# Reciprocal square roots in fewer operations, and the decay output's root and gate applied from PSUM: a two-block transformer kernel in float32 on one core

## The chip, the cores and the metric

One core of one Trainium2 chip. The time is the device time of one execution in microseconds (us). Of the kernel before there are three timed runs and one profiled execution, whose rows are shown further down.

## The reference

A hidden state of 512 tokens by 1024 goes through two blocks of two layers each, all in float32. A layer of the first block is cut here to what the change touches:

```python
def _rms(x, g=None):
    y = x * lax.rsqrt(jnp.mean(x * x, axis=-1, keepdims=True) + EPS)
    return y if g is None else y * g

h = _rms(x, norm_g[l])
proj = h @ w_in[l]                       # 9304 columns, split into the parts
...
o = jnp.einsum('bnchk,bnhkv->bnchv', q, states)      # decay branch: 4 heads of 128
o = _rms(o, norm_g)                                  # gain gla_norm_g[l], 128 numbers
y_a = o * jax.nn.silu(gz)
y_b = _dsa(_rms(bq, dsa_qn_g), _rms(bk, dsa_kn_g), ...) * jax.nn.silu(bz)
y_c = _rms(diff_attention) * (1 - lambda_init) * jax.nn.silu(cz)
merged = sum(sigmoid(gate[m]) * (y_m @ w_br[l, m]) for m in (a, b, c))
x = x + merged @ w_out[l]
```

The decay branch is a linear attention with one state for each chunk of 64 tokens, its output normed over the 128 elements of each head. The second branch attends to the 128 best keys of each query, the third is a difference of two softmaxes. A layer of the second block has a modulated norm, a mixer with compressed, selected and windowed attention beside a pooling branch, then a second modulated norm and a feed-forward of width 4096. Its queries and keys are normed by heads of 64 too. So there are roots of the following kinds: of a whole token row (six norms: two of the first block, four of the second), of 4, 8 or 16 heads of a token tile (queries and keys of all layers), of the 4 heads of the outputs `y_a` and `y_c`, and of the compressed keys.

## The kernel before, in words

**Tiles and precision.** The 512 tokens are four tiles of 128. Each large product is made from float32 values split into a high and a low half, as three matrix products: high by high, low by high, high by low. Weights come in pieces of 512 KB. SP issues the DMA of a piece into `raw` (a ring of 6), ACT copies its high half into `wh` (line 1355, a ring of 5), POOL subtracts to give the low half `wl` (line 968, eight instructions of 128x128 for each slab of the piece), and PE sweeps it (line 1037). POOL does nothing else.

**Order.** Each engine runs its own list of steps. The lists are written by hand, as the strings `FIRST` and `SECOND` and a table `MOVED` for each engine; none of these is in the diff. Steps wait for each other through semaphores: an instruction that somebody waits for gets a key (`mark`), and the other engine waits for the key's count (`at`, `place`). DVE waits for its own last count (`now`) between two instructions of which the second reads what the first wrote. PSUM banks go round in rings (`BANK_RINGS`), and a product waits for `("free", ...)`, the last reader of the bank's earlier user. `ROOTS` is bank 7.

**Norm of a token row: the steps `scale` and `turn`.** Tiles are normed in two pairs, p0 (tiles 0 and 1) and p1 (2 and 3). ACT sums the squares into `stat[:, 7, 0:4]` (line 1470). In `scale`, DVE makes v (line 1882) and a first guess by integer arithmetic on the bits (1885), then three rounds, in which each of the two columns is its own instruction on one column, with both multipliers given as per-partition scalars (1891, 1896), and a last factor (1899), which is the key `root`. ACT waits for it and scales the even tile (line 1481); DVE scales the odd tile (1903). PE turns the scaled tiles (line 991), DVE applies gain and modulation (1918 to 1925), ACT takes the high half `hTh` (1489) and DVE the low half `hTl` (1929); PE's sweeps wait for these. The text calls a norm by its stage: n0, n1 (first block), a0, a1 (second block, first norm), f0, f1 (second block, before the feed-forward).

**Roots by heads.** `rsqrt` (lines 1686 to 1702) makes a guess, a half of v, and three rounds of three operations, from and to small tiles in SBUF (`nsm`); where it is given a room in PSUM, the root of each round lies there (line 1944, and the compressed keys).

**The decay output: the step `y_tok.a`.** For one token tile, PE leaves the 4 heads in two banks, the even heads 0 and 2 in one and the odd heads 1 and 3 in the other (line 1139). ACT squares both into SBUF (line 1539, one instruction for each bank). DVE sums the squares by heads (2054), makes v (2057), the root (`rsqrt`: 1690, 1693, and 1696, 1698, 1700 three times), the factor 0.5 (2063), multiplies the PSUM banks by z, twice the gate's silu (2071, two instructions), by the root (2076) and by the norm's gain (2081). Then PE turns y (line 991, in the step `y_turn`), ACT takes its high half `yTh` (1550), DVE its low half `yTl` (2087), and the next tile's product may use the banks.

## Time and profile before

| what | value |
| --- | --- |
| three timed runs | 2504.82, 2506.04 (median) and 2506.5 us |
| the profiled execution's own time | 2507.29 us |
| its span (first to last instruction) | 2505.5 us |
| granted TensorE clock, mean of the span | 0.994 |
| PE busy | 2414.9 us, 96% |
| DVE busy | 1365.2 us, 54% |
| ACT busy | 934.5 us, 37% |
| POOL busy | 1289.0 us, 51% |

The profiled execution is 1.25 us above the median of the timed runs; 1.8 us of it lie outside the span. In rows of the timeline the first number is the start in us from the span's start, the second the length from the first to the last end of what the row groups. Then come engine, line, operation, what it writes <- what it reads, sizes and types, and "x" with the number of instructions. In square brackets stand the engine's idle time just before and what ended it. In the rows of waits "17.2, 3, 6.9" means 17.2 us in total, 3 times, the longest 6.9 us. A view of one line gives least, median and greatest duration in ns, then first and last start.

### The profile page before, as it was taken

Reading aid. Unit: us, or ns where it says so; the run is one execution under the profiler, and the core shown is the slowest. Engines: PE = TensorE matmul, PEld = TensorE weight load, DVE = VectorE, ACT = ScalarE, POOL = GpSimd, SP = SyncE. Lnnn points to the kernel's source line nnn. Section 1 sums busy time; section 2 is a strip of 40 time slices with the busy share of each in tenths; the row PEclk is TensorE's granted clock in tenths of the full one; section 3 lists DMA queues with packets and bytes.
Section 4 is the critical chain, followed back from the end, with each engine's and each line's share of the span. In section 5 each row is a group of like instructions: output and inputs, shape, how many; then the busy total and the mean of one; then the engine's idle time right before and its main releaser. Section 6 shows DMA issues by size and latency. Waiting matters only on the chain. (4 is left out here: it accounts for less than half of the span.)

```text
span 2505.5 us, 36332 instructions
## 1 busy us (share of the span) xinstructions
PE 2414.9 (96%) x12167; PEld 1936.7 (77%) x12171; DVE 1365.2 (54%) x2819; ACT 934.5 (37%) x1691; POOL 1289.0 (51%) x2900
## 2 busy tenths in 40 slices
PE   6999999999999999999999998999999999899999
PEld 5777878788877777878888667777788856788887
DVE  5487453654448755355467646543658663522325
ACT  4433343432443334343244743222224473332221
POOL 4455644546545564454555214576774422555663
PEclk9999999999999999999999999999999999999999
DMA  5322423235422242323542112434543201232332
GB/s 167 92 68 84 145 92 109 93 97 177 154 86 72 81 152 92 118 76 102 179 121 64 43 34 77 167 125 146 177 139 96 74 27 41 81 99 92 102 108 78
DMA packets 132815, 258.26 MB, mean 103 GB/s; under 512 B 21994, under 2 KB 28700, under 8 KB 132636
## 3 DMA queue, kind: packets, MB, share of 16 engines
q1 hardware_dynamic: 132636, 255.94, 32.5%
q8 instruction: 104, 1.70, 0.3%
q14 instruction: 75, 0.61, 0.1%
HBM read 251.70 MB, written 4.21 MB: 102 GB/s over the span
## 5 line engine op out<-in xcount | busy, mean ns | idle before, releaser
L968 POOL TENSOR_TENSOR wl<-raw,wh 128x128 fp32r<-128x128 f32 (+2 forms) x2896 | 1288.8, 485 | 1191.1 <-ACT wh L1355 1190.6
L1037 PE MATMUL ps<-wh,hTh 128*128 128x512 f32 (+3 forms) x1600 | 633.0, 396 | 5.8 <-DVE hTl L2305 3.0
L1037 PE MATMUL ps<-wh,hTl 128*128 128x512 f32 (+3 forms) x1600 | 613.7, 384 | 0.0
L1037 PE MATMUL ps<-wl,hTh 128*128 128x512 f32 (+3 forms) x1600 | 612.7, 383 | 0.0
L1355 ACT ACTIVATE wh<-raw 128x1024 fp32r<-128x1024 f32 (+2 forms) x362 | 372.2, 1047 | 434.8 <-PE ps L1037 306.0
L1037 PEld LDWEIGHTS ps<-wh,hTh 128*128 128x128 f32 x1600 | 302.6, 189 | 77.7 <-issue 23.3
L1037 PEld LDWEIGHTS ps<-wh,hTl 128*128 128x128 f32 x1600 | 301.7, 189 | 57.4
L1037 PEld LDWEIGHTS ps<-wl,hTh 128*128 128x128 f32 x1600 | 302.7, 189 | 49.4
L1037 PE MATMUL ps<-hTh,wh 128*128 128x512 f32 (+2 forms) x704 | 260.9, 371 | 15.2 <-DVE hTl L1929 6.7
L1037 PE MATMUL ps<-hTh,wl 128*128 128x512 f32 (+2 forms) x704 | 258.8, 368 | 0.0
L1037 PE MATMUL ps<-hTl,wh 128*128 128x512 f32 (+2 forms) x704 | 258.8, 368 | 0.0
L2123 DVE SCALAR_TENSOR_TENSOR modw<-modw,cact 128x1024 f32<-128x1024 f32 x96 | 165.4, 1734 | 105.4 <-DMA modw<-in_w_mod_dram 104.7
L1037 PE MATMUL ps<-wh,yTh 128*128 128x512 f32 x448 | 176.8, 395 | 4.2 <-POOL wl L968 1.6
L1037 PE MATMUL ps<-wh,yTl 128*128 128x512 f32 x448 | 174.7, 390 | 0.0
L1037 PE MATMUL ps<-wl,yTh 128*128 128x512 f32 x448 | 174.6, 390 | 0.0
L1037 PEld LDWEIGHTS ps<-hTh,wh 128*128 128x128 f32 (+1 forms) x704 | 133.1, 189 | 45.0 <-issue 12.2
L1037 PEld LDWEIGHTS ps<-hTl,wh 128*128 128x128 f32 (+1 forms) x704 | 133.1, 189 | 21.6
L1037 PEld LDWEIGHTS ps<-hTh,wl 128*128 128x128 f32 (+1 forms) x704 | 133.1, 189 | 20.8
L991 PE MATMUL ps<-cf,arena 128*128 128x128 f32 x704 | 106.8, 287 | 24.9 <-ACT arena L1481 17.2
L1764 DVE TENSOR_TENSOR arena<-ps,arena 128x512 f32<-128x512 f32 x80 | 55.2, 690 | 122.1 <-PE ps L1037 118.9
L991 PEld LDWEIGHTS ps<-cf,arena 128*128 128x128 f32 x704 | 85.8, 147 | 44.8 <-ACT arena L1481 19.3
L1749 DVE TENSOR_SCALAR scr<-ps 128x512 f32<-128x512 f32 (+1 forms) x72 | 44.9, 624 | 131.3 <-PE ps L1037 131.3
(274 smaller groups left out, 3136.1 us busy)
## 6 DMA issues: line engine op xcount, KB each, us to landing
raw<-in_w_in_dram SPq DMA_DIRECT2D x160, 512.0 KB, 3.6
raw<-in_w_ff_dram SPq DMA_DIRECT2D x128, 512.0 KB, 3.7
modw<-in_w_mod_dram SPq DMA_DIRECT2D x96, 512.0 KB, 4.7
raw<-in_w_br_dram SPq DMA_DIRECT2D x24, 512.0 KB, 3.7
raw<-in_w_out_dram SPq DMA_DIRECT2D x24, 512.0 KB, 3.8
xm<-in_x_dram SPq DMA_DIRECT2D x8, 512.0 KB, 4.7
raw<-in_w_out_dram SPq DMA_DIRECT2D x16, 256.0 KB, 3.8
raw<-in_w_in_dram SPq DMA_DIRECT2D x8, 408.0 KB, 3.3
```

The source lines that it names most:

```text
L968: last = pool.tensor_tensor(low[part], whole[part], high[part], ALU.subtract)
L991: last = pe.transpose(dst[:, c * P:(c + 1) * P], src[:, c * P:(c + 1) * P], ident)
L1037: last = pe.matmul(*args, start=(q == 0 and c == 0 and n_pass == 0), stop=(q == u["quarters"] - 1 and c == u["chunks"] - 1 and n_pass == 2))
L1355: act.activation(piece(wh, g % SPLIT, u), piece(raw, g % RING, u), ACT.Copy)\
L1749: dve.tensor_scalar(tmp, b, 0.0, None, ALU.max).then_inc(dve_result, mark(dve_result))
L1764: dve.tensor_tensor(acc, b, acc, ALU.add).then_inc(dve_result, mark(dve_result, free))
L2123: dve.scalar_tensor_tensor(w, w, 0.5, cact[:], ALU.mult, ALU.mult, accum_out=modT[:, m // MOD_STEPS, m % MOD_STEPS:m % MOD_STEPS + 1])\
```

## The change

The diff touches five places.

1. `scale`: the twelve one-column instructions and the last factor are replaced by `rsqrt_short` on both columns at once: a guess, then two rounds of four operations (a product, and three operations that multiply or add a constant and multiply). The constants of the last factor go into v. The root is left in `stat[:, 7, 4:8]`, where ACT and DVE read it.
2. The norms of queries and keys in the first block (`rstd`) and of the third branch's output (`y_tok.c`) use `rsqrt_short` too, with their factor folded into v.
3. `rsqrt_wide` takes the place of `rsqrt` for the heads of the second block, the compressed keys and `y_tok.a`: three rounds as before, but the half of v is made in the instruction that made v, and the root of each round lies in PSUM.
4. `y_tok.a`: ACT squares head by head and leaves the four sums in `stat[:, 6]` (accum_out), so DVE's sum is gone; the factor 0.5 is folded into v; root and z are applied in one instruction for each head, from PSUM.
5. The gain of the decay branch's norm becomes a column of `colT`, and is applied in `y_turn`, by ACT's scale and by DVE's scalar, to the turned y. The gain's own tile and its DMA at the start are gone.

The diff, cut:

```diff
-        def y_parts(step):
+        def gla_head(step, h):
             _, l, m, t = step
...
+            head = slice(h * P, (h + 1) * P)
+            return (y_at(l, m, t)[:, head], ps[:, bank_of.get((("gla_out", l, t), h % 2), 0), (h // 2) * P:(h // 2 + 1) * P],
+                    z_[m][:, t, head])
...
-                    act.activation(xn[:, 0], xm[:, 2 * pair], ACT.Copy, scale=nsm[:, 3, 0:1])\
+                    act.activation(xn[:, 0], xm[:, 2 * pair], ACT.Copy, scale=stat[:, 7, 4 + 2 * pair:5 + 2 * pair])\
...
-                        for y, b, _ in y_parts(step):
-                            ins = act.activation(y, b, ACT.Square)
+                        for h in range(4):
+                            y, b, _ = gla_head(step, h)
+                            ins = act.activation(y, b, ACT.Square, accum_out=stat[:, 6, 4 * t + h:4 * t + h + 1])
...
-                                   ACT.Copy).then_inc(act_result, mark(act_result, ("yh", step)))
+                                   ACT.Copy, scale=col("gla_norm", l) if m == "a" else 1.0)\
+                        .then_inc(act_result, mark(act_result, ("yh", step)))
...
+            def rsqrt_short(y, v, *keys):
+                m, n = v.shape[0], v.shape[-1]
+                root, tmp, ratio = nsm[0:m, 1, 0:n], nsm[0:m, 2, 0:n], nsm[0:m, 3, 0:n]
                 dve.tensor_scalar(root.bitcast(I32), v.bitcast(I32), -0.5, float(0x5f3759df), ALU.mult, ALU.add)\
...
+                for r in range(2):
+                    dve.tensor_tensor(tmp, root, root, ALU.mult).then_inc(dve_result, mark(dve_result))
...
+                    dve.scalar_tensor_tensor(ratio, tmp, SHORT ** r, v, ALU.mult, ALU.mult).then_inc(dve_result, mark(dve_result))
...
+                    dve.scalar_tensor_tensor(tmp, ratio, -10.0 / 3.0, ratio, ALU.add, ALU.mult)\
...
+                    dve.scalar_tensor_tensor(y if r == 1 else root, tmp, 5.0, root, ALU.add, ALU.mult)\
+                        .then_inc(dve_result, mark(dve_result, *(keys if r == 1 else ())))
...
-                    for r, three in enumerate((3.0, 12.0, 768.0)):
-                        for k in range(2):
-                            one = slice(k, k + 1)
-                            dve.wait_ge(dve_result, at("guess", step, r, k))
-                            dve.tensor_scalar(w[:, one], y[:, one], y[:, one], v[:, one], ALU.mult, ALU.mult)\
-                                .then_inc(dve_result, mark(dve_result, ("ratio", step, r, k)))
-                        for k in range(2):
...
-                            dve.tensor_scalar(y[:, one], w[:, one], -three, y[:, one], ALU.add, ALU.mult)\
...
-                    dve.tensor_scalar(nsm[:, 3, 0:1], y[:, 0:1], -1.0 / 8192.0, None, ALU.mult)\
-                        .then_inc(dve_result, mark(dve_result, ("root", step)))
+                    v, y = nsm[:, 0, 0:2], stat[:, 7, 4 + 2 * pair:6 + 2 * pair]
+                    dve.tensor_scalar(v, stat[:, 7, 2 * pair:2 * pair + 2], 1.0 / D / SHORT ** 2, EPS / SHORT ** 2,
+                                      ALU.mult, ALU.add).then_inc(dve_result, mark(dve_result))
+                    dve.wait_ge(dve_result, now(dve_result))
+                    rsqrt_short(y, v, ("root", step))
...
+                        dve.wait_ge(act_result, at("osq", step))
+                        half = nsm[:, 2, 0:4]
+                        dve.tensor_scalar(half, stat[:, 6, 4 * t:4 * t + 4], 0.5 / 0.25 / P, 0.5 * EPS / 0.25, ALU.mult, ALU.add)\
...
+                        rsqrt_wide(nsm[:, 1, 0:4], half, ps[:, bank_of.get((("gla_out", l, t), 0), 0), 256:260])
+                        for h in (0, 2, 1, 3):
+                            part, b, z = gla_head(step, h)
+                            dve.scalar_tensor_tensor(part, b, nsm[:, 1, h:h + 1], z, ALU.mult, ALU.mult)\
+                                .then_inc(dve_result, mark(dve_result, *([("free", (("gla_out", l, t), h % 2))] if h > 1 else []),
+                                                           *([("y_tok", l, m, t)] if h == 3 else [])))
...
-                        g = glag[:, l].unsqueeze(1).to_broadcast([P, 4, P])
-                        dve.tensor_tensor(y3, y3, g, ALU.mult).then_inc(dve_result, mark(dve_result, ("y_tok", l, m, t)))
...
-                    dve.tensor_tensor(yTl[:, :, tile], ps[:, bank_of.get(step, 0)].rearrange("p (c n) -> p c n", c=4),
-                                      yTh[:, :, tile].bitcast(F32), ALU.subtract)\
+                    dve.scalar_tensor_tensor(yTl[:, :, tile], ps[:, bank_of.get(step, 0)].rearrange("p (c n) -> p c n", c=4),
+                                             col("gla_norm", l) if m == "a" else 1.0, yTh[:, :, tile].bitcast(F32),
+                                             ALU.mult, ALU.subtract)\
```

PE's list is the same, 9813 rows in the same order; DVE's goes from 2184 rows to 2102. Two places on DVE show what the prediction speaks of. The first is the step `scale` of one pair; `nsm` and `stat` are small tiles in SBUF, `arena` holds the scaled tile. Before:

```order
L1882 TENSOR_SCALAR nsm<-stat 128x2
L1885 TENSOR_SCALAR nsm<-nsm 128x2
L1891 TENSOR_SCALAR nsm<-nsm 128x1 x2
L1896 TENSOR_SCALAR nsm<-nsm 128x1 x2
L1891 TENSOR_SCALAR nsm<-nsm 128x1 x2
L1896 TENSOR_SCALAR nsm<-nsm 128x1 x2
L1891 TENSOR_SCALAR nsm<-nsm 128x1 x2
L1896 TENSOR_SCALAR nsm<-nsm 128x1 x2
L1899 TENSOR_SCALAR nsm<-nsm 128x1
L1903 TENSOR_SCALAR arena<-xm,nsm 128x1024
```

and of the change:

```order
L1896 TENSOR_SCALAR nsm<-stat 128x2
L1703 TENSOR_SCALAR nsm<-nsm 128x2
L1707 TENSOR_TENSOR nsm<-nsm 128x2
L1709 SCALAR_TENSOR_TENSOR nsm<-nsm 128x2
L1711 SCALAR_TENSOR_TENSOR nsm<-nsm 128x2
L1714 SCALAR_TENSOR_TENSOR nsm<-nsm 128x2
L1707 TENSOR_TENSOR nsm<-nsm 128x2
L1709 SCALAR_TENSOR_TENSOR nsm<-nsm 128x2
L1711 SCALAR_TENSOR_TENSOR nsm<-nsm 128x2
L1714 SCALAR_TENSOR_TENSOR stat<-nsm 128x2
L1901 TENSOR_SCALAR arena<-xm,stat 128x1024
```

Fifteen instructions ahead of the scaling have become ten, and eight of the ten take two operands from SBUF. The second place is `y_tok.a` of one token tile; `ps` is PSUM, `scr` holds y, `arena` holds z. Before:

```order
L2054 TENSOR_REDUCE nsm<-scr 128x4
L2057 TENSOR_SCALAR nsm<-nsm 128x4
L1690 TENSOR_SCALAR nsm<-nsm 128x4
L1693 TENSOR_SCALAR nsm<-nsm 128x4
L1696 TENSOR_TENSOR nsm<-nsm 128x4
L1698 TENSOR_TENSOR nsm<-nsm 128x4
L1700 SCALAR_TENSOR_TENSOR nsm<-nsm 128x4
...
L2063 TENSOR_SCALAR nsm<-nsm 128x4
L2071 TENSOR_TENSOR scr<-ps,arena 128x2x128 x2
L2076 TENSOR_TENSOR scr<-scr,nsm 128x512
L2081 TENSOR_TENSOR scr<-scr,glag 128x512
```

and of the change:

```order
L2067 TENSOR_SCALAR nsm<-stat 128x4
L1687 TENSOR_SCALAR ps<-nsm 128x4
L1691 TENSOR_TENSOR nsm<-ps,nsm 128x4
L1693 TENSOR_TENSOR nsm<-nsm,ps 128x4
L1695 SCALAR_TENSOR_TENSOR ps<-nsm,ps 128x4
...
L1691 TENSOR_TENSOR nsm<-ps,nsm 128x4
L1693 TENSOR_TENSOR nsm<-nsm,ps 128x4
L1695 SCALAR_TENSOR_TENSOR nsm<-nsm,ps 128x4
L2073 SCALAR_TENSOR_TENSOR scr<-ps,nsm,arena 128x128 x4
```

The three rounds stand once in the first piece and as their first and last in the second. The sum of the squares, the separate half of v, the factor 0.5 and two passes over 512 elements have gone, and every operation of the rounds has one operand in PSUM.

## Rows read from the trace of the kernel before

**Rows 1.** The page's first part: busy time of each engine in the whole span.

```profile
PE 2414.9 (96%) x12167; PEld 1936.7 (77%) x12171; DVE 1365.2 (54%) x2819; ACT 934.5 (37%) x1691; POOL 1289.0 (51%) x2900
```

**Rows 2.** What PE waited for: total us, times, longest us.

```profile
PE ps L991 <- ACT arena L1481: 17.2, 3, 6.9
...
PE ps L1037 <- DVE hTl L1929: 8.2, 5, 2.4
...
PE ps L991 <- DVE scr L2081: 3.9, 4, 1.5
...
PE ps L1139 <- DVE scr L2071: 1.8, 2, 0.9
...
PE ps L991 <- DVE yTl L2087: 0.9, 1, 0.9
```

**Rows 3.** Timeline of the decay output in layer 0, one tile.

```profile
236.78 0.66 ACT L1539 ACTIVATE scr<-ps 128x256 f32<-128x256 f32 x2 [8.35 <-PE ps L1139]
...
237.56 0.69 DVE L2054 TENSOR_REDUCE nsm<-scr 128x4 f32<-128x512 f32 x1 [0.55 <-ACT scr L1539]
...
238.46 5.89 POOL L968 TENSOR_TENSOR wl<-raw,wh 128x128 fp32r<-128x128 f32 x14 [7.42 <-ACT wh L1355]
...
239.40 0.38 DVE L1696 TENSOR_TENSOR nsm<-nsm 128x4 f32<-128x4 f32 x1
...
245.34 0.82 DVE L2081 TENSOR_TENSOR scr<-scr,glag 128x512 f32<-128x512 f32 x1
```

**Rows 4.** Two lines apart: durations, least/median/greatest in ns, by operands.

```profile
L1696 DVE TENSOR_TENSOR nsm<-nsm x60: 161/184/390, 115.1 to 1172.1; 128x4 f32<-128x4 f32 x48, 128x16 f32<-128x16 f32 x6, 128x32 f32<-128x32 f32 x6
L1696 DVE TENSOR_TENSOR nsm<-ps,nsm x30: 147/166/175, 1304.5 to 1978.9; 128x8 f32<-128x8 f32 x12, 128x16 f32<-128x16 f32 x12, 32x2 f32<-32x2 f32 x6
L1981 DVE SCALAR_TENSOR_TENSOR xm<-ps,arena,xm x56: 350/547/752, 87.7 to 783.9; 128x128 f32<-128x128 f32 x14, 128x256 f32<-128x256 f32 x14, 128x384 f32<-128x384 f32 x14, 128x512 f32<-128x512 f32 x14
```

**Rows 5.** Timeline of ACT: a 128x128 activation from PSUM that leaves its sum.

```profile
309.23 0.45 ACT L1561 ACTIVATE arena<-ps,soft,stat 128x128 f32<-128x128 f32 x1
```

**Rows 6.** Stretch after a stall: start:end, us, engines' busy time, PEclk, DMA share, GB/s.

```profile
246.30:252.00 5.70, 5.69 (x21) 4.81 (x22) 5.12 (x19) 0.25 (x1) 0.00 (x0) 0.74 0.01 1
```

**Rows 7.** Timeline of PE after the decay output of layer 1.

```profile
893.05 0.47 PE L1037 MATMUL ps<-wh,hTh 128*128 128x512 f32 x1 [1.19 <-issue]
```

**Rows 8.** Timeline of the norm a0, pair p1.

```profile
1289.76 0.17 DVE L1885 TENSOR_SCALAR nsm<-nsm 128x2 int32<-128x2 int32 x1
...
1291.80 0.14 DVE L1899 TENSOR_SCALAR nsm<-nsm 128x1 f32<-128x1 f32 x1
...
1293.18 2.15 PE L991 MATMUL ps<-cf,arena 128*128 128x128 f32 x11 [4.43 <-ACT arena L1481]
```

**Rows 9.** Timeline of the norm n0, pair p1.

```profile
11.07 17.09 POOL L968 TENSOR_TENSOR wl<-raw,wh 128x128 fp32r<-128x128 f32 x40 [10.63 <-ACT wh L1355]
...
22.00 6.18 DVE L1882 TENSOR_SCALAR nsm<-stat 128x2 f32<-128x2 f32 x1
```

**Rows 10.** Timeline of the norm f0, both pairs.

```profile
1513.69 0.39 DVE L1885 TENSOR_SCALAR nsm<-nsm 128x2 int32<-128x2 int32 x1
...
1516.15 1.15 ACT L1481 ACTIVATE arena<-xm,nsm 128x1024 f32<-128x1024 f32 x1 [1.91 <-DVE nsm L1899]
...
1518.02 0.71 PE L991 MATMUL ps<-cf,arena 128*128 128x128 f32 x5
...
1527.10 6.72 POOL L968 TENSOR_TENSOR wl<-raw,wh 128x128 fp32r<-128x128 f32 x16 [4.22 <-ACT wh L1355]
...
1530.95 0.38 DVE L1885 TENSOR_SCALAR nsm<-nsm 128x2 int32<-128x2 int32 x1
...
1542.13 0.36 PE L1037 MATMUL ps<-hTh,wh 128*128 128x256 f32 x1 [2.42 <-DVE hTl L1929]
```

**Rows 11.** Timeline of the norm n1, pair p1.

```profile
663.28 1.15 ACT L1481 ACTIVATE arena<-xm,nsm 128x1024 f32<-128x1024 f32 x1 [1.81 <-DVE nsm L1899]
...
664.49 1.75 PE L991 MATMUL ps<-cf,arena 128*128 128x128 f32 x14
```

More of the change, by code:

```diff
@@ L2062, in _ @@
-                        scale = 0.5 if m == "a" else 0.5 * (0.2 + 0.6 * float(np.exp(-0.3 * l)))
-                        dve.tensor_scalar(nsm[:, 1, 0:4], nsm[:, 1, 0:4], scale, None, ALU.mult)\
+                        rsqrt_short(nsm[:, 1, 4:8], nsm[:, 0, 0:4])
+                        y3 = y.rearrange("p (h d) -> p h d", h=4)
+                        dve.tensor_tensor(y3, y3, nsm[:, 1, 4:8].unsqueeze(2).to_broadcast([P, 4, P]), ALU.mult)\
+                            .then_inc(dve_result, mark(dve_result, ("y_tok", l, m, t)))
@@ new lines, in _ @@
+                        dve.wait_ge(dve_result, now(dve_result))
+                    elif m == "b":
+                        for key in y_free(step):
+                            dve.wait_ge(*place(key))
+                        dve.tensor_tensor(y, ps[:, bank_of.get(("value", l, m, t), 0)], z_[m][:, t], ALU.mult)\
+                            .then_inc(dve_result, mark(dve_result, ("free", ("value", l, m, t)), ("y_tok", l, m, t)))
+                        dve.wait_ge(dve_result, now(dve_result))
+                    else:
+                        dve.wait_ge(act_result, at("osq", step))
+                        half = nsm[:, 2, 0:4]
+                        dve.tensor_scalar(half, stat[:, 6, 4 * t:4 * t + 4], 0.5 / 0.25 / P, 0.5 * EPS / 0.25, ALU.mult, ALU.add)\
@@ L2064, in _ @@
                             .then_inc(dve_result, mark(dve_result))
                         dve.wait_ge(dve_result, now(dve_result))
-                    if m != "c":
-                        for key in y_free(step):
-                            dve.wait_ge(*place(key))
-                        for n, (part, b, z) in enumerate(y_parts(step)):
-                            key = ("free", (("gla_out", l, t), n) if m == "a" else ("value", l, m, t))
-                            dve.tensor_tensor(part, b, z, ALU.mult)\
-                                .then_inc(dve_result, mark(dve_result, key, *([("y_tok", l, m, t)] if m == "b" else [])))
-                            dve.wait_ge(dve_result, now(dve_result))
```

95 lines of the change are left out of this document (35 added, 60 removed).

## The prediction

> **What bounds the kernel now.** I read the busy times first, then what PE waited for, then the timeline around each wait that a changed line ends. PE is busy in 96% of the span and DVE in 54% [rows 1]. So 82 fewer DVE instructions are worth nothing by their number; they are worth what they shorten of the times at which PE stands. The change touches three kinds of such times: PE waits for the scaled token tiles, 17.2 us in three waits; for the low half of the normed state, 8.2 us in five; and for the decay output, 3.9, 1.8 and 0.9 us [rows 2]. Everything else of PE's time is products that stay as they are, in the same order.
>
> The second thing to read is what a small DVE operation costs. With both operands in SBUF it takes between 161 and 390 ns; with one of them in PSUM it takes 147 to 175 [rows 4]. In the timeline the 0.38 us stand inside a run of POOL's subtractions [rows 3]. One operation follows the other after about 0.20 us when POOL is idle and 0.42 when it is busy (length plus some 35 ns). I read this as DVE and POOL sharing a way to SBUF that a second SBUF operand needs. It decides the sign of each term below.
>
> **The decay output (`y_tok.a`), with a gain.** Before, from the start of the squares at 236.78 to the end of the last multiplication at 245.34 + 0.82 = 246.16 it takes 9.4 us, with POOL busy [rows 3]. After:
> - ACT squares four heads in place of two banks. An activation of 128x128 from PSUM that leaves its sum takes 0.45 [rows 5]: 1.8 us for 0.66.
> - DVE's sum (0.69) is gone. The v and the guess are 0.2 each, nine operations with one PSUM operand 0.2 each, for which the upper row is 0.175 long [rows 4]: 2.2 us.
> - Four multiplications from PSUM. The form with a PSUM and an SBUF operand takes 0.35 at its least, which is 128 columns wide [rows 4]: 1.4 us. Three whole passes of 512 (0.69 to 0.83) are gone.
>
> That is 5.4 us for 9.4, and it no longer depends on POOL. With POOL idle the old chain was, from the same lengths, 0.7 for the squares, 0.7 for the sum, 13 x 0.2 for the small ones and 2.3 for the four passes, together 6.3, so there about 0.9 us are gained. The waits to be covered are at most 1.5 us (for y) where POOL is busy, 0.48 us where it is idle, and 0.9 us (for the banks, whose last reader comes sooner too, by over 2 us). All are covered. In layer 0 the waits are 0.48, 0.89 and 1.47, in sum 2.8. In layer 1 they are 0.47, 0.89 and 1.47 of the same kinds, 0.9 for `yTl`, which was late because the step before it was, and 1.2 behind it [rows 2, 7], in sum 4.9. (The split by layer is mine: of the 3.9 us in four waits two are 1.5, the others share 0.9.) After the last wait of layer 0 the granted clock is 0.74 for 5.7 us [rows 6]; at full speed the same work takes 0.26 x 5.7 = 1.5 us less, and with no stall ahead I expect it there. **Sum -9.2 us.** Bounds: nothing, if the PE waits are ended by something that stood just behind these; and -9.2, since no more was waited for. I take the full value, as the margins (4.0, 2.3 and 0.9 us) exceed each wait.
>
> The gain moved into `y_turn` adds no instruction; ACT and DVE read one more column there. I cost it at nothing; a few tens of ns would be hidden by sweeps between turn and use. The dropped DMA at the start lies behind others that PE waits for longer, also nothing.
>
> **The token-row norms (`scale`), gains where POOL is idle.** In a0 p1 the guess starts at 1289.76 and the last factor ends at 1291.80 + 0.14 = 1291.94, 2.18 us later [rows 8]. After it there are one guess and eight operations of 0.2: 1.76. So 0.43 us are gained, straight off the wait of 4.43 us that follows. The same in a1 p1 (5.9 of the 17.2 us: 17.2 - 6.9 - 4.4) and n0 p1 (6.9). **Sum -1.3 us.** The bounds for each: -0.5, if the operations take the 161 ns of [rows 4] and follow at once, and 0.
>
> **The same, losses where POOL is busy.** The old one-column operations, whose multipliers come as scalars, were not slowed by POOL. The eight new ones take two SBUF operands each, so each takes 0.42 where POOL is busy: 0.42 x 9 = 3.74 us from the guess on.
> - f0 p0: the guess starts at 1513.69, and the root is there at 1516.15, 2.4 us later; the guess's 0.39 tells that POOL is busy [rows 10]. After: +1.3. The scaled tile is ready at 1516.15 + 1.15 = 1517.30 and PE takes it at 1518.02, without a wait. So 0.7 of the 1.3 are hidden in that slack, and 0.6 are not. Twice, for f1 has the same order: +1.2.
> - f0 p1: PE waits 2.4 us for `hTl` behind it [rows 10], so all of a delay counts. The guess starts at 1530.95 and POOL's run ends at 1533.82 [rows 10]: 2.87 us hold the guess and six of the eight operations, the other two take 0.2. The root comes 3.3 us after the guess, for 2.4: +0.85. The bounds are +1.3, if all eight are slowed, and -0.4, if none. Twice: +1.7.
> - n1 p1: the scaled tile is ready at 663.28 + 1.15 = 664.43 and PE starts on it at 664.49 [rows 11]. There is next to no slack: +1.2.
> - p0 of n0: slower by up to 1, but PE waits for p1 after it anyway, and p1's wait is set by something else (below). Nothing.
>
> **Sum +4.1 us.** Where this cover is gone, nothing further is late. In `rstd` and `y_tok.c` 13 operations become 10, all with SBUF operands as before; they are at most 0.8 us each and PE doesn't wait for them beyond 0.1 to 0.3 us in all: -0.2. `rsqrt_wide` for the second block's heads saves one operation of each root, off the path: 0.
>
> **Sum of all:** -9.2 - 1.3 + 4.1 - 0.2 = -6.6 us. Against the profiled execution's own 2507.29 that is 2500.7; the median of the runs is 1.25 lower, so for the median I forecast 2506.04 - 6.6 = **2499.4 us**. What a measurement of this kernel can tell from no change is about 0.2%, 5.0 us: faster means below 2501.0, slower above 2511.1.
>
> **Rivals.**
>
> *The long hold at the start does not come back.* In n0 p1 one operation on two columns takes 6.18 us, from 22.00 to the end of POOL's run at 28.16 [rows 9]. None of the 60 executions of line 1696 was held so long [rows 4], so it depends on how the two meet. In this pair DVE's instructions in front of it are shifted by the new roots of p0. If it takes 0.4, the roots of p1 run beside POOL and are ready at about 22.4 + 3.7 = 26.1, in place of 28.2 + 0.2 + 1.8 = 30.2; of the 6.9 us of PE's wait 4 go, giving 2495.4. The Trainium skill, page "SBUF — State Buffer", section "Who interferes with whom", says that DVE and GpSimd share one pair of ports, and that whoever issues first has it for the whole instruction while the other fully blocks. By that rule the operation should wait for one POOL instruction at the longest, and this rival would be the normal case; the trace shows 6.18 us for it, so here the trace does not agree. For the rival: most others were not held. Against: DVE reaches it back to back behind a long operation, and still will.
>
> *Most of the decay gain fails to come.* ACT is the engine that gets more work there (1.8 us for 0.7), in the same list as the high halves of the weights. If `wh` comes later for it, or if the waits are passed on to the next product in the ring, half of the 9.2 us stays: 2499.4 + 4.6 = 2504.0. For it: ACT's copies are in line with PE's sweeps. Against: ACT is busy 37% of the time [rows 1], and the ring holds several pieces.
>
> *Nothing moves.* The roots are no longer, and no shorter, than what they replace, and the waits go to neighbours: 2506. The margins above speak against it.
>
> *Slower: the new operations at the heads of the norms get held.* The mechanism is that of [rows 9]: an SBUF operation of DVE that meets a run of POOL's waits for the end of the run. A `scale` had two operations of two columns before, now it has ten. A hold costs 3 to 6 us and falls straight on PE where p1 or a tight p0 is held. From three such holds on it decides: 2499.4 + 3 x 5 = 2514.4. For it: the form is the one that shares something with POOL. Against: rows of 390 ns are the longest of 60 executions of such an operation [rows 4]; none was held.
>
> **How the numbers follow.** Forecast as summed 0.45; the start's hold gone 0.23; half of the decay gain 0.22; nothing moves 0.05; slower 0.05. The forecast's own uncertainty comes from the unknown terms: f0, f1 and n1 between -0.4 and +1.3 for each root, 2 us to either side of the sum, so 2497 to 2502. The range goes to the two next cases, 2495.4 less 2 at the low end and 2504.0 plus 0.5 at the high one: 2493.5 to 2504.5, which leaves the two last cases and some tails out. Faster by over 0.2%: 0.38 of the 0.45 and all of the 0.23, 0.61. Within: 0.07 + 0.22 + 0.05 = 0.34. Slower: 0.05.
>
> **What would show it.** In the profile after, the waits of PE for `scr`, for line 1139's banks and for `yTl` must be gone, and the small operations of `y_tok.a` 0.15 to 0.18 us long even inside POOL's runs. The wait for the scaled tiles goes from 17.2 to about 16. The roots of f0 p0 take 3.7 us from the guess for 2.4, PE gets a wait of about 0.6 there, n1 one of about 1.2, and the waits for `hTl` grow by 0.85 each. Wrong would be: waits of the same size under other names behind the decay output; a clock no better after it; or operations of `scale` beside POOL at 0.2 us, which would take the +4.1 away.

## The result, and the profile after

The changed kernel takes **2491.97 us** (median of 4 runs, 2488.26 to 2495.51); the kernel before 2505.7 (4 runs, 2504.82 to 2506.5). The ratio is 0.9948, with a 95% interval of 0.9935 to 0.996, so 13.7 us faster by the medians where 6.6 were forecast, and 1.5 us below the low end of the range. The profiled execution took 2491.42 us; its span is 2489.5, 16.0 less than before.

The page's busy times of the kernel after answer to [rows 1]:

```profile
PE 2411.7 (97%) x12171; PEld 1935.1 (78%) x12171; DVE 1316.3 (53%) x2681; ACT 939.0 (38%) x1739; POOL 1286.8 (52%) x2900
```

PE's own work is the same within 3.2 us; DVE has 49 us less, of which 16 came through. What PE waits for after the change, first rows of the view (us in total, times, longest), against [rows 2]:

```profile
PE ps L986 <- ACT arena L1476: 18.0, 7, 5.8
...
PE ps L1032 <- DVE hTl L1927: 10.1, 7, 3.1
```

The waits for `scr`, for the decay output's banks and for `yTl` have no row any more. The wait for the scaled tiles has grown by four short waits (18.0 in seven, for 17.2 in three), and the one for `hTl` by 1.9 us, as forecast for the norms beside POOL (+1.7).

Since PE runs the same matmuls in the same order, the two traces can be laid side by side, and each place at which the distance between them changes is a place at which time was gained or lost. The table is worked out so, from the starts of matmuls in both; times in the first column are those of the kernel before.

| place (us) | what PE waited for there | measured | forecast |
| --- | --- | --- | --- |
| 31.65 | norm n0, pair p1, net of +0.4 in p0 | -0.6 | -0.4 |
| 31.7 to 37.7 | the clock behind it | -1.1 | 0 |
| 237, 244, 246 to 249 | decay output, layer 0, with the clock behind | -0.5, -1.0, -2.9 | -4.3 |
| 336 | probability of the second branch | -0.7 | 0 |
| 483, 1109 | probability of the third branch | -1.1, -1.2 | -0.2 |
| 608, 1235 | low half of the merged state, the end of both first-block layers | -1.5, -1.5 | 0 |
| 664 | norm n1 | +1.3 | +1.2 |
| 863, 870, 872, 893 | decay output, layer 1 | -0.5, -1.0, -1.5, -2.5 | -4.9 |
| 1293 | norm a0, p1 (its wait 4.43, now 3.97) | -0.5 | -0.4 |
| 1293 to 1298 | the clock behind it | +0.8 | 0 |
| 1518, 1543 | norm f0 | +0.7, +1.0 | +1.4 |
| 1909 | norm a1 | -0.7 | -0.4 |
| 2132, 2157 | norm f1 | +0.7, +0.6 | +1.4 |

The large terms of the forecast's sum came out within 0.7 us each. What was not in it: 7.1 us of gain in four rows (the clock behind n0, 336 us, the third branch, the ends of the layers) for which it had 0.2, and 0.8 of loss in the clock behind a0. Some 2.4 us more of gain are in smaller steps, in which a step of -0.9 at 1562 and one of +0.9 at 1579 cancel. The two rows that name the clock are not shown to be the work of the change, as the other traces tell further down.

**The decay output.** The tile of [rows 3] in the timeline of the kernel after, DVE and ACT (start, length, engine, line, operation):

```profile
234.66 0.28 ACT L1535 ACTIVATE scr<-ps 128x128 f32<-128x128 f32 x1 [7.86 <-PE ps L1134]
...
235.93 0.17 DVE L2067 TENSOR_SCALAR nsm<-stat 128x4 f32<-128x4 f32 x1 [3.40 <-ACT scr L1535]
...
236.82 5.05 POOL L963 TENSOR_TENSOR wl<-raw,wh 128x128 fp32r<-128x128 f32 x12 [7.89 <-ACT wh L1350]
...
237.72 0.16 DVE L1693 TENSOR_TENSOR nsm<-nsm,ps 128x4 f32<-128x4 f32 x1
...
238.10 1.13 DVE L2073 SCALAR_TENSOR_TENSOR scr<-ps,nsm,arena 128x128 f32<-128x128 f32 x4
```

From the first square to y it is 239.23 - 234.66 = 4.6 us, where 9.4 were needed before and 5.4 estimated. An operation of the rounds takes 0.16 in the middle of POOL's run. ACT's four squares with their sums follow each other every 0.26 us, not 0.45 as I took from [rows 5], and the four multiplications take 1.13, not 1.4. The stretch after, of the same length as the one of [rows 6] (start:end, us, busy times, PEclk, DMA share, GB/s):

```profile
242.80:248.50 5.70, 5.70 (x39) 4.38 (x38) 4.38 (x17) 1.14 (x6) 0.75 (x2) 1.00 0.32 95
```

The granted clock is 1.00 for 0.74 before, and 39 matmuls stand in it for 21. But the kernel before does not always pay this. In its second profiled execution (see the experiments) PE waits the same 1.47 us there, and the stretch of 5.7 us behind the wait has a clock of 1.00:

```profile
244.94:250.64 5.70, 5.70 (x27) 4.79 (x28) 5.12 (x19) 0.24 (x1) 0.00 (x0) 1.00 0.21 48
```

So 1.4 of the 2.9 us are gained only against executions in which the clock falls. Of the five traces here with the old step it fell in three (0.72 to 0.74), and in none of the seven with the new one.

**The token-row norm beside POOL.** The norm f0 of [rows 10] in the timeline after:

```profile
1494.90 8.18 POOL L963 TENSOR_TENSOR wl<-raw,wh 128x128 fp32r<-128x128 f32 x18 [7.27 <-ACT wh L1350]
...
1496.26 0.39 DVE L1703 TENSOR_SCALAR nsm<-nsm 128x2 int32<-128x2 int32 x1
...
1498.36 0.39 DVE L1707 TENSOR_TENSOR nsm<-nsm 128x2 f32<-128x2 f32 x1
...
1500.03 1.15 ACT L1476 ACTIVATE arena<-xm,stat 128x1024 f32<-128x1024 f32 x1 [3.22 <-DVE stat L1714]
...
1501.24 1.97 PE L986 MATMUL ps<-cf,arena 128*128 128x128 f32 x16 [0.49 <-ACT arena L1476]
```

Guess to root takes 3.77 us (forecast 3.74) for 2.46, and PE has a wait of 0.49 where it had none.

**The ends of the first-block layers.** Here stands the largest part that I had not seen. In the timeline of the kernel before:

```profile
600.77 5.89 POOL L968 TENSOR_TENSOR wl<-raw,wh 128x128 fp32r<-128x128 f32 x14
...
601.73 6.01 DVE L2123 SCALAR_TENSOR_TENSOR modw<-modw,cact 128x1024 f32<-128x1024 f32 x1
...
607.67 1.88 DVE L2314 SCALAR_TENSOR_TENSOR hTl<-ps,hTh 128x512 fp32r<-128x512 f32 x3
608.40 0.66 PE L991 MATMUL ps<-cf,xm 128*128 128x128 f32 x4 [1.25 <-DVE hTl L2314]
```

and of the kernel after:

```profile
593.13 1.44 DVE L2118 SCALAR_TENSOR_TENSOR modw<-modw,cact 128x1024 f32<-128x1024 f32 x1
...
595.58 1.29 DVE L2309 SCALAR_TENSOR_TENSOR hTl<-ps,hTh 128x512 fp32r<-128x512 f32 x2 [1.00 <-ACT hTh L1676]
```

An operation on a modulation weight, which nobody waits for, was held until POOL's run was over, 6.0 us for 1.2; behind it in DVE's list stands the low half of the merged state, for which PE waits. It looks like the hold of [rows 9] at another place. After the change it is not held, and PE's 1.25 us wait is gone with it; the distance between the traces grows by 1.5, and by 1.5 again at the twin of layer 1. There it is POOL that gives way:

```profile
593.43 1.45 POOL L963 TENSOR_TENSOR wl<-raw,wh 128x128 fp32r<-128x128 f32 x1
```

Its neighbours in the run take 0.46 to 0.47 us.

### The profile page after: what moved, and what is told of

Its sections match the earlier page's. It is cut to its first block and busy times, and to the rows that moved or that the text cites. A ratio compares the mean times of both kernels' runs of the same rounds, so it can differ in the third digit from the quotient of the medians.

```text
span 2489.5 us, 36237 instructions
## 1 busy us (share of the span) xinstructions
PE 2411.7 (97%) x12171; PEld 1935.1 (78%) x12171; DVE 1316.3 (53%) x2681; ACT 939.0 (38%) x1739; POOL 1286.8 (52%) x2900
## 5 line engine op out<-in xcount | busy, mean ns | idle before, releaser
L2118 DVE SCALAR_TENSOR_TENSOR modw<-modw,cact 128x1024 f32<-128x1024 f32 x96 | 156.5, 1641 | 107.4 <-DMA modw<-in_w_mod_dram 106.7
```

The source lines that it names most:

```text
L2118: dve.scalar_tensor_tensor(w, w, 0.5, cact[:], ALU.mult, ALU.mult, accum_out=modT[:, m // MOD_STEPS, m % MOD_STEPS:m % MOD_STEPS + 1])\
```

## The experiments

Two questions were open. Which part brought the 7 us more than forecast, and are the holds part of the program or chance? All ratios are to the kernel before, measured beside each run on the same chip; its median there is given, since it lies between 2504.1 and 2507.3. Where a loss or gain is given "at" a place, it is again a step in the distance between two traces.

### The parts one by one

**`y_tok.a` alone.** The changed kernel with `scale`, `rstd` and `y_tok.c` as before:

```diff
-                    rsqrt_short(y, v, ("root", step))
+                    for r, three in enumerate((3.0, 12.0, 768.0)):
...
-                    rsqrt_short(s, v, *([("rstd", l, name)] if name[1] == "q" else []))
+                    if name[1] == "q":
+                        rsqrt(nsm[:, 1, 0:4 * nh], v)
...
-                        rsqrt_short(nsm[:, 1, 4:8], nsm[:, 0, 0:4])
+                        rsqrt(nsm[:, 1, 0:4], nsm[:, 0, 0:4])
+                        dve.tensor_scalar(nsm[:, 1, 4:8], nsm[:, 1, 0:4], scale, None, ALU.mult)\
```

> Parts 4 and 5 of the change alone (the decay output's step, and the roots by heads of the second block), with the old scale, the old roots of queries and keys and the old roots of the third branch's output. My theory: the step gives what it gave in the changed kernel, 4.4 us in layer 0 and 5.4 in layer 1, so about 2496 us; PE's waits of 0.96 for the third branch's probabilities, at about 475 and 1095 us, stay, since the roots ahead of them are as long as before. Rival: the 7 us more than forecast come from the long holds of DVE (6 us operations beside POOL), which any shift of the instructions releases; then this kernel too lies near 2492, without the holds at 602 and 1228 us.

Measured: 2495.81 us (2489.14 to 2497.25) against 2507.31, ratio 0.9944 (0.9924 to 0.9965). Laid beside the kernel before, the decay output gives -4.4 and -5.6 us, the same as in the changed kernel. The waits for the third branch's probabilities stay, one row in the waits of PE:

```profile
PE ps L986 <- DVE arena L2153: 1.9, 2, 1.0
```

The time is what my theory gave, but the rival is right too in one point: the holds at 602 and 1228 us are gone (-1.5 each). The executions differ as well: the profiled one is the fastest of the four (2489.14), and in it neither of two operations of another line is held (`cmp_in`, line 2180 before; -3.1 us where layer 0's was held before).

**`scale` alone**, put into the kernel before:

```diff
-                    for r, three in enumerate((3.0, 12.0, 768.0)):
...
+                    rsqrt_short(y, v, ("root", step))
```

> Part 1 alone, put into the kernel before: rsqrt_short in the token-row norms. My theory: slower by about 3 us (2508.5): n1 +1.3, f0 +1.7, f1 +1.5, less 0.4 each for the pairs p1 of a0, a1 and n0. Rival (any shift releases holds): the gain of 3.5 us at the ends of the two first layers comes here too and outweighs it, 2505 or less.

Measured: 2511.46 us (2505.27 to 2514.79) against 2507.31, ratio 1.0011 (0.9999 to 1.0023). By itself this part makes the kernel slower, or at best no faster: n1 +1.3, f0 +0.7 and +0.3, f1 +0.7 and +0.6. The holds at 602 and 1228 are gone here too (-1.5 each), and one at `cmp_in` of layer 1 stands in this trace (+3.0).

**`rstd` and `y_tok.c` alone**, put into the kernel before:

```diff
...
+                    rsqrt_short(s, v, *([("rstd", l, name)] if name[1] == "q" else []))
...
+                        root = nsm[:, 1, 4:8] if m == "c" else nsm[:, 1, 0:4]
+                        if m == "c":
+                            rsqrt_short(root, nsm[:, 0, 0:4])
...
```

> Part 2 alone, put into the kernel before: rsqrt_short for the norms of queries and keys of the first block and for the third branch's output. My theory: the waits of 0.96 us for the probabilities at 483 and 1109 us, behind a chain of roots beside POOL that is three operations of 0.42 shorter, go; -2.2 us in all, 2503.5. If these waits are ended by something else, nothing moves: 2505.7.

Measured: 2503.98 us (2499.62 to 2506.15) against 2507.31, ratio 0.9981 (0.9971 to 0.999): -3.3 by the medians, -4.8 by the ratio. The two waits for probabilities have no row in the waits of PE any more, -1.1 and -1.2 at their places. The holds at 602 and 1228 are gone (-1.5 each), and the one at `cmp_in` of layer 1 stands here too (+3.0).

**The changed kernel with the old `scale`:**

```diff
-                    rsqrt_short(y, v, ("root", step))
+                    for r, three in enumerate((3.0, 12.0, 768.0)):
...
```

> The changed kernel with the old one-column scale put back. My theory: the losses at n1, f0 and f1 (4.5 us) go and about 1 us of gains at a0, a1 and n0 goes too: 2488.5, 3.5 us below the changed kernel. Rival (the new scale costs nothing beside POOL, and its place in time is what matters): 2492, as the changed kernel.

Measured: 2491.81 us (2489.35 to 2492.72) against 2507.31, ratio 0.9932 (0.9916 to 0.9949). By the medians as the changed kernel; by the ratios 0.16% better, with intervals that overlap. The number is that of the rival, while the places are those of my theory: beside the kernel before there is no loss at n1, f0 and f1 (in the changed kernel 4.3 us), but in this trace the layer-1 hold at `cmp_in` costs 2.5 us, and a lower granted clock behind a wait for `wl` near 1690 us costs 1.8. So the loss is shown at its places, and not in the time of the whole.

### Are the holds chance?

**Both kernels profiled a second time.**

> The kernel before, profiled a second time. If the long holds of DVE are a property of the program, the same ones stand in the same places: 6.2 us at 22.0, 6.0 at 310, 6.0 at 602 and 1228, 4.7 at 1334 and none at 1952. If they differ from execution to execution, one or more of the last four is gone or new, and the span moves by 1.5 to 3 us for each.

> The changed kernel, profiled a second time. What the change itself gives must stand in both profiles: the waits behind the decay output gone, n1, f0 and f1 later by 1.3, 1.7 and 1.5 us. The gains of 1.7 us at the ends of the two first layers, if they are chance, need not.

Measured: 2517.36 and 2491.11 us, one execution each. The change's own gains and losses stand in both traces of the kernel after, but for the second place of f0. From 1520 to 1550 us (times of the kernel before) the first trace is later by 0.6 (+1.0 at 1542, -0.4 behind it), the second by 0.3, and 0.3 is also what two kernels with the old `scale` have there (part 2 alone, and the one with v by single columns). In these three PE's products ahead of the wait take 1.5 us longer, and the wait behind them is shorter by most of it. So the loss at f0 p1 is shown in one trace of two. The kernel before, second execution, has three new long holds. One is in the decay output (+3.5 us behind it):

```profile
258.87 4.68 POOL L968 TENSOR_TENSOR wl<-raw,wh 128x128 fp32r<-128x128 f32 x11
259.50 4.60 DVE L2076 TENSOR_TENSOR scr<-scr,nsm 128x512 f32<-128x512 f32 x1
...
265.61 0.66 PE L991 MATMUL ps<-cf,scr 128*128 128x128 f32 x4 [2.38 <-DVE yTl L2087]
```

one is at `cmp_in` of layer 1 (+3.0), and one is a small operation in front of the window attention, an operation on 8 columns that took 5.3 us and 7.0 of PE's time:

```profile
1418.82 0.41 DVE L2271 TENSOR_REDUCE csoft<-arena 128x8 f32<-128x256 f32 x1
1419.26 0.20 DVE L2273 RECIPROCAL csoft<-csoft 128x8 f32<-128x8 f32 x1
1419.49 5.30 DVE L2275 TENSOR_TENSOR csoft<-csoft,gts 128x8 f32<-128x8 f32 x1
```

So there are two kinds. Some holds recur: n0 p1 in all traces of both kernels; an operation of the second branch near 310 us (6.0 us for 0.3) and modulation operations near 935, 1563, 1684 and 1766 us in every one of the twelve traces here; 602 and 1228 in both traces of the kernel before and in none of the two of the kernel after, nor in any of the other kernels here. Others come by the execution: `cmp_in` in layer 0 and in layer 1 (each held in 1 of 2 traces of the kernel after; in ten and in eight of the twelve traces), line 2076, line 2275. In the first pair of traces `cmp_in` of layer 1 was free on both sides. The kernel before ran from 2502.1 to 2514.4 us here, and steps of 3 to 7 us behind such holds are of the size of this spread; which of them stood in an unprofiled run is not known. Line 2076 of `y_tok.a` is an operation that the change removes, and with it its holds; it was held in one of two traces of the kernel before, and once more in the kernel of the next part.

What decides on a hold I could not settle. At 602 us the operation starts 116 ns after POOL's began in the first trace of the kernel before, where it was held, and 117 ns in the trace of the kernel after, where it was not (110 ns in the second trace of the kernel before, held, and 110 at 1229 us in the kernel of the next part, not held); POOL's run had been going for 5.16 us in all of them.

The clock is a second thing that changes from trace to trace. Behind a0, PE's wait is 3.97 us both in the changed kernel and with `scale` alone, and the granted clock of the 5.1 us after it is 0.50 in the first and 0.69 in the second:

```profile
1275.50:1280.60 5.10, 5.10 (x22) 5.10 (x23) 3.54 (x6) 1.90 (x3) 2.92 (x8) 0.50 0.07 12
1290.10:1295.20 5.10, 5.10 (x27) 5.10 (x28) 3.53 (x6) 1.92 (x3) 2.93 (x8) 0.69 0.08 13
```

With the old wait of 4.43 us it is 0.67 in both traces of the kernel before and 0.50 in `y_tok.a` alone and with the old `scale`. Behind n0 p1, where PE waits 6.9 us, the two executions of the kernel before differ by 0.9 us. So the loss of 0.8 us behind a0 and the gain of 1.1 behind n0 in the table are not shown to come from the change.

**Which operations are held.** The kernel before, v by one column each:

```diff
-                    dve.tensor_scalar(v, stat[:, 7, 2 * pair:2 * pair + 2], 1.0 / D, EPS, ALU.mult, ALU.add)\
-                        .then_inc(dve_result, mark(dve_result))
+                    for k in range(2):
+                        dve.tensor_scalar(v[:, k:k + 1], stat[:, 7, 2 * pair + k:2 * pair + k + 1], 1.0 / D, EPS, ALU.mult, ALU.add)\
+                            .then_inc(dve_result, mark(dve_result))
```

> The kernel before; only the first operation of each scale (v, two columns) is done as two operations of one column. Theory 1, on n0 p1: what is held to the end of POOL's run is a form that takes the shared way, which an operation on one column does not; then no 6.2 us there, the roots of p1 are ready some 4 us sooner and PE's wait of 6.9 shrinks to about 2.5: -4 to -5 us with the clock. Rival: v is held all the same, and nothing moves at the start. Theory 2, on the holds at 602 and 1228 us: they hang on chance in the exact sequence, so they are gone here too as in the four other programs (-1.7 us each); rival: they belong to the kernel before as long as none of the three parts is in it, and stay. Together between 2507 and 2498.

Measured: 2504.76 us (2497.17 to 2511.29) against 2504.09, ratio 1.0004 (0.9993 to 1.0015). The timeline of n0 p1:

```profile
22.24 0.20 DVE L1883 TENSOR_SCALAR nsm<-stat 128x1 f32<-128x1 f32 x2
22.48 5.97 DVE L1886 TENSOR_SCALAR nsm<-nsm 128x2 int32<-128x2 int32 x1
28.48 0.45 DVE L1892 TENSOR_SCALAR nsm<-nsm 128x1 f32<-128x1 f32 x2
```

The two operations of one column run freely, and the next one, of two columns, is held in their place. Both of my alternatives for it were too simple: v is not held, and still nothing moves. The holds at 602 and 1228 are gone here too (-1.5 each), in a kernel in which nothing but this was changed. So they belong to the exact program, and I can't say to which property of it. The time of the whole did not fall with them: in this trace line 2077 (2076 before) and `cmp_in` of layer 1 are held, at 3.8 and 3.0 us.

### The place of the roots

**The rounds of `y_tok.a` in SBUF:**

```diff
-                        rsqrt_wide(nsm[:, 1, 0:4], half, ps[:, bank_of.get((("gla_out", l, t), 0), 0), 256:260])
+                        rsqrt_wide(nsm[:, 1, 0:4], half, nsm[:, 1, 4:8])
```

> The changed kernel with the rounds' root of y_tok.a in SBUF in place of PSUM, nothing else. My theory: beside POOL each of the ten operations takes 0.42 for 0.20 us, so y comes 2.2 us later there; the waits for the banks (0.96 before) come back with about 0.8 us in each layer, those for y hardly: 2493 to 2494, and a y_tok.a operation that is held for 3 to 5 us may stand in the profile. Rival (the place of the root does not matter, what gave the gain is the passes removed): 2492 and all ten at 0.2 us or with no wait of PE behind them.

Measured: 2493.1 us (2491.67 to 2494.36) against 2504.09, ratio 0.9955 (0.9939 to 0.9972). The operations beside POOL are slowed, as expected:

```profile
238.07 0.16 DVE L1695 SCALAR_TENSOR_TENSOR nsm<-nsm 128x4 f32<-128x4 f32 x1
238.27 0.37 DVE L1691 TENSOR_TENSOR nsm<-nsm 128x4 f32<-128x4 f32 x1
238.67 0.39 DVE L1693 TENSOR_TENSOR nsm<-nsm 128x4 f32<-128x4 f32 x1
```

but PE has no wait behind them in either layer; the expected 0.8 us in each did not come. Here the rival is right: the gain is that of the passes and sums that went, and the root's place in PSUM is not needed for it. POOL's run begins in the midst of the chain, so that in this tile only six of its small operations are slowed, and the chain has margin.

**The token-row roots with PSUM operands**, in the changed kernel:

```diff
-                    v, y = nsm[:, 0, 0:2], stat[:, 7, 4 + 2 * pair:6 + 2 * pair]
+                    if (stage, pair) != (('n', 0), 0):
+                        dve.wait_ge(dve_result, now(dve_result))
+                    v, y = ps[:, ROOTS, 64:66], stat[:, 7, 4 + 2 * pair:6 + 2 * pair]
...
-                    rsqrt_short(y, v, ("root", step))
+                    rsqrt_half(y, v, ps[:, ROOTS, 66:68], ("root", step))
...
+            def rsqrt_half(y, half, tmp, *keys):
+                m, n = half.shape[0], half.shape[-1]
+                root = nsm[0:m, 1, 0:n]
+                dve.tensor_scalar(root.bitcast(I32), half.bitcast(I32), -0.5, float(0x5f3759df - (1 << 22) - (1 << 31)),
+                                  ALU.mult, ALU.add).then_inc(dve_result, mark(dve_result))
+                dve.wait_ge(dve_result, now(dve_result))
+                for r in range(3):
+                    dve.tensor_tensor(tmp, root, half, ALU.mult).then_inc(dve_result, mark(dve_result))
...
+                    dve.tensor_tensor(tmp, tmp, root, ALU.mult).then_inc(dve_result, mark(dve_result))
...
+                    dve.scalar_tensor_tensor(y if r == 2 else root, tmp, -1.5, root, ALU.add, ALU.mult)\
```

> The changed kernel, with the roots of the token rows in three rounds of the wide form, in which v and the product lie in PSUM and the root in SBUF: every small operation has at most one SBUF operand. My theory (the second SBUF operand is what is slowed beside POOL): each takes 0.2 us also there, so n1, f0 and f1 lose their 4.5 us, and the 6.2 us hold of n0 p1 is gone, 4 us more: 2483 to 2484. Rival (the hold is not a matter of operands): the operation that makes v in n0 p1 is still held to the end of POOL's run, 2487.

Measured: **2487.79 us** (2485.99 to 2491.91) against 2506.88, ratio 0.9928 (0.9913 to 0.9943). The number is that of the rival, and its condition did not come: v is not held. The time is below both kernels by the medians, 4.2 us below the changed one; by the ratios the intervals overlap a little (0.9935 to 0.9943). Norm f0, beside POOL:

```profile
1490.57 7.62 POOL L963 TENSOR_TENSOR wl<-raw,wh 128x128 fp32r<-128x128 f32 x17 [7.30 <-ACT wh L1350]
...
1491.82 0.16 DVE L1703 TENSOR_SCALAR nsm<-ps 128x2 int32<-128x2 int32 x1
...
1493.61 0.16 DVE L1711 SCALAR_TENSOR_TENSOR stat<-ps,nsm 128x2 f32<-128x2 f32 x1
...
1496.26 1.91 PE L986 MATMUL ps<-cf,arena 128*128 128x128 f32 x16
```

Guess to root is 1.95 us for 3.77, and PE has no wait. Norm n0, pair p1:

```profile
22.00 0.16 DVE L1914 TENSOR_SCALAR ps<-stat 128x2 f32<-128x2 f32 x1
...
23.98 0.16 DVE L1711 SCALAR_TENSOR_TENSOR stat<-ps,nsm 128x2 f32<-128x2 f32 x1
24.18 4.59 DVE L1919 TENSOR_SCALAR arena<-xm,stat 128x1024 f32<-128x1024 f32 x1
...
28.82 1.09 PE L986 MATMUL ps<-cf,arena 128*128 128x128 f32 x8 [1.28 <-DVE arena L1919]
```

None of the eleven small operations is held. The next one with an operand and a result in SBUF, the scaling of the odd tile, is, for 4.6 us; but ACT's even tile is ready meanwhile, and of PE's 5.8 us there 1.3 are left in that row. Beside the changed kernel the start is 5.1 us shorter, with the clock behind it, n1 1.6, f0 1.3 and f1 1.8, as forecast. Four losses come off: the layer-1 hold at `cmp_in` (2.4); 1.5 at 604 us and 2.1 at 1763, where DVE waits 2.3 and 2.7 us for the DMA of a modulation weight; and 1.6 behind the wait for `wl` near 1690 us, which is of the same length in both (1.84 us in the changed kernel, 1.80 here), but has a clock of 1.00 behind it in the one and of 0.57 in the other:

```profile
1687.60:1691.60 4.00, 4.00 (x17) 3.27 (x18) 1.44 (x3) 0.60 (x1) 3.26 (x8) 1.00 0.34 131
1681.80:1685.80 4.00, 4.00 (x11) 3.13 (x12) 1.37 (x2) 0.00 (x0) 3.23 (x8) 0.57 0.29 112
```

So 2.5 us are left in the two spans.

**And the roots of `y_tok.c` in PSUM**, in the bank of that output:

```diff
...
-                        dve.tensor_reduce(nsm[:, 0, 0:4], squares.rearrange("p (h d) -> p h d", h=4), AX, ALU.add)\
+                        dve.tensor_reduce(value[:, 0:4], squares.rearrange("p (h d) -> p h d", h=4), AX, ALU.add)\
...
-                        rsqrt_short(nsm[:, 1, 4:8], nsm[:, 0, 0:4])
+                        rsqrt_half(nsm[:, 2, 4:8], value[:, 0:4], value[:, 4:8], ("free", ("value", l, m, t)))
...
```

> As the run before it, and the roots of the third branch's output in PSUM too, in the bank of that output, which comes free some 3 us later for it. My theory: its roots beside POOL get 2 us shorter, but the wait for the probabilities is gone already; a further gain of 0 to 1 us. Rival: the bank, the only one of its ring, comes free too late and PE waits for it: slower by 1 us and more in each of up to eight tiles.

Measured: 2489.11 us (2487.72 to 2491.33) against 2506.88, ratio 0.9934 (0.9917 to 0.995): nothing gained. The rival is right in three tiles: at the products into that bank PE now waits for the last root, and is later by 0.7 at 464 us, 0.7 at 1084 and 1.4 at 1111. And behind the first of them the multiplication by the root is held, so that the wait for the probability is back, +1.7 at 470 us:

```profile
464.14 5.32 DVE L2074 TENSOR_TENSOR arena<-arena,nsm 128x512 f32<-128x512 f32 x1
...
471.83 0.41 PE L986 MATMUL ps<-cf,arena 128*128 128x128 f32 x2 [1.49 <-DVE arena L2131]
```

## Why the prediction was wrong

**What was right.** The direction, and what bounds the kernel. The decay output: -9.2 forecast, -9.9 measured, at the places named and with the clock back at 1.00; 1.4 of it, the clock, the kernel before lost in its first profiled execution and not in its second. Single terms in it were off in length (0.26 for 0.45, 0.28 for 0.35) with no effect, since the chain had margin. That PSUM operands would be needed for it was implied by "it no longer depends on POOL", and the experiment says that they are not. The losses beside POOL: +4.1 forecast, +4.3 measured (the chain of nine was 3.77 us long for 3.74, though 0.42 x 9 as written is 3.78). The gains at n0, a0 and a1: -1.3 forecast, -1.8 measured. One sign was at odds with the forecast's own sum: the wait for the scaled tiles was to fall to about 16, but the new waits at n1, f0 and f1 stand in the same row, and it rose to 18.0. And the reading that a second SBUF operand is what is slowed beside POOL is too narrow for its own rows: the guess has one input, in SBUF, and took 0.39 us beside POOL [rows 10], and v, with one input too, is what was held [rows 9]. With input or result in PSUM both took 0.16 beside POOL.

**The step that failed first** is the sentence "they are at most 0.8 us each and PE doesn't wait for them beyond 0.1 to 0.3 us in all: -0.2". There the chain was not followed to its end. Three operations fewer are 3 x 0.42 = 1.26 us beside POOL, and five instructions behind the multiplication of `y_tok.c` stands the probability for which PE waited 0.96 us, twice. The row was in the view of waits of the kernel before, under the line of the probability, and I had read that view only for lines that the diff names:

```profile
PE ps L991 <- DVE arena L2117: 1.9, 2, 1.0
```

The first of the two in the timeline, from the end of the roots to PE:

```profile
479.57 0.39 DVE L2063 TENSOR_SCALAR nsm<-nsm 128x4 f32<-128x4 f32 x1
480.00 0.90 DVE L2076 TENSOR_TENSOR arena<-arena,nsm 128x512 f32<-128x512 f32 x1
...
482.65 0.48 DVE L2117 SCALAR_TENSOR_TENSOR arena<-arena,soft 128x256 f32<-128x256 f32 x1
...
483.28 0.41 PE L991 MATMUL ps<-cf,arena 128*128 128x128 f32 x2 [0.96 <-DVE arena L2117]
```

So the term is -2.3 us where the forecast had -0.2, and part 2 alone takes these 2.3 us.

**The second** is that holds were priced only where one could come or go at a changed line. The rival had the mechanism, at the wrong place, and with 0.23: the hold in n0 p1 stayed in every trace but those in which its operation was changed, and there it went on to the next one of its kind. The holds that went are those at 602 and 1228 us, 2.9 us in this trace, in an operation that the diff doesn't touch. All nine other programs here, even one with a single operation split, are without them. Since the kernel before is the one program that has them, a change to it gains these 2.9 us at their places by being a change. The time of the whole does not show it: with v by single columns the ratio is 1.0004, as other holds stood there. Their length stood in the profile (6.0 us for 1.2, with a wait of PE behind it), and a forecast should have asked what a shift does to them.

**What is left** was no step of the forecast. The -1.1 behind n0 p1 is the clock of one execution: `y_tok.a` alone and the kernel with the old `scale`, in which PE waits 6.9 us there as before, have -1.4 and -1.3, the second execution of the kernel before has -0.9, and `scale` alone, with the new roots, has nothing. The -0.7 at 336 us stands in all three partial kernels (-0.4 to -0.7), and I have no cause for it.

**The rivals.** Most of the decay gain failing to come, nothing moving, and new holds at the heads of the norms did not occur. Of the last, the price of 3 to 6 us was too narrow: on PE's path a hold cost 1.5 us (602), 3.0 (`cmp_in`), 3.5 (line 2076) and 7.0 (line 2275). That the median fell below the range is so in part the -0.2 that was 2.3, in part the holds; how much of the 7 us is chance of the executions on both sides these four runs each can't tell.

**What stays open.** What decides on a hold, what sets the clock behind a stall of a given length, and the smaller steps (2.4 us). By the parts, -11.5, +4.2 and -3.3 us of their medians make -10.7, where the whole is -13.7 to its own reference; by the ratios they are -14.0, +2.8 and -4.8, together -16.0, for -13.0. Each of the parts contains the missing holds at 602 and 1228, so their sum counts these three times, and holds of 3 us that come by the execution lie in all.

## What to carry to other kernels

Where an operation gets shorter, go through the whole list of waits of the bounding engine and ask of each row whether the shortened one stands somewhere ahead of it in its engine's list, and not only whether its line is named. Count operations by their operands and not by their number: ten, of which eight had two SBUF operands, were slower beside a busy GpSimd (POOL) than fifteen, of which thirteen worked on one column, and eleven with v and the product in PSUM were faster than either. And where one kernel's trace has operations many times as long as their kind, take a second trace of it before a difference is read as the work of a change. The same goes for a difference in the clock.

## What the runs showed of the hardware that was not expected

- A DVE operation on small tiles with two SBUF operands takes 0.38 us beside a run of GpSimd and 0.16 without; with one of them in PSUM 0.16 in both. The guess, with a single input, is slowed in the same way when input and result lie in SBUF (0.38 for 0.17), and not when one of them is in PSUM (0.16 to 0.17). An operation on a single column is not slowed either (0.20 us for two, where the next on two columns took 5.97).
- The same kinds of operation are sometimes held until GpSimd's whole run ends: 4.6 us (128x512), 5.3 (128x8), 6.2 (128x2), up to 12.7 for one of 128x1024. Whether it happens differs between programs and, at some places, between executions of one program. Between programs the starts agree within 1 ns in their position to GpSimd's operation (116 and 117 ns at 602 us). Where the 128x1024 operation was not held, one instruction of GpSimd took 1.45 us for 0.47. The Trainium skill, page "SBUF — State Buffer", section "Who interferes with whom", has one engine blocked for the other's whole instruction; the slowing to 0.38 us and the 1.45 us of GpSimd's instruction agree with that, and the holds over ten and more instructions do not.
- ACT's 128x128 square with a sum follows every 0.26 us from PSUM, where the exponential with a sum and operands read from `soft` and `stat`, [rows 5], is 0.45 long.
- Stalls of the same length at the same place had different clocks behind them: 0.74 and 1.00 in two executions of one kernel behind 1.47 us (5.7 us after the decay output's last wait); 0.67 and 0.50 in two kernels behind 4.43 us, 0.69 and 0.50 behind 3.97 us (5.1 us after the wait at a0); 1.00 and 0.57 behind 1.84 and 1.80 us (4.0 us near 1690).
